# In-projection of a mixer layer: gate tiles first, convolution taps moved, first short taps on ScalarE

## What is computed

```python
h = rmsnorm(x, mix_norm[i]) @ w_in[i]            # 14 tiles of 128 columns in the kernel
y_mla  = mla_mixer(h[q 256], h[kv 128], h[k_pe 32])     # 8 heads of softmax attention
y_conv = conformer_conv_mixer(h[conv 512])       # a * sigmoid(g), depthwise conv of 31 taps, layernorm, silu
y_hy   = hyena_mixer(h[hy 768])                  # depthwise conv of 3 taps, two long convolutions by FFT
y = concatenate([rmsnorm(y_mla), rmsnorm(y_conv), rmsnorm(y_hy)])
x = x + y @ w_out[i]

# in mla_mixer
q  = rmsnorm(h_q, q_norm) @ w_qb
kv = rmsnorm(h_kv, kv_norm) @ w_kvb
```

## Time and profile before

| | |
|---|---|
| median of 3 runs | 3381.22 us (3379.67 to 3386.06) |
| the profiled execution's own time | 3378.02 us |
| its span, first to last instruction | 3376.2 us |
| busy: PE, DVE, ACT, POOL | 97%, 53%, 22%, 54% |
| in-projection and heads of layer 1 | 412 to 670 us of the span |
| the same of layer 2 | 1478 to 1737 us |

### The profile page before, as it was taken

The page is one execution under the profiler, slowest core; times in us unless marked ns, Lnnn a source line. Parts: engine busy times, 40 slices in busy tenths (PEclk is TensorE's granted clock), DMA queues, the critical chain, the costliest instruction groups (busy, mean ns, idle before and its releaser), DMA issues.

```text
span 3376.2 us, 43947 instructions
## 1 busy us (share of the span) xinstructions
PE 3259.0 (97%) x14466; PEld 2576.2 (76%) x14466; DVE 1803.6 (53%) x1969; ACT 744.3 (22%) x1260; POOL 1834.1 (54%) x1026
## 2 busy tenths in 40 slices
PE   8999998999999999999889999999999999999998
PEld 6788874478888788886457888788777777888886
DVE  7552268663312755138855331587768886753312
ACT  2110115522201111013532220111122322222200
POOL 5556651056666646663026666644455555666665
PEclk9999999999999999999999999999999999999999
DMA  4223320023233322331012232322222222223232
GB/s 156 79 76 99 112 81 26 7 82 99 94 99 98 111 75 88 100 110 59 13 33 93 94 99 95 120 75 69 69 85 66 73 68 75 90 91 99 94 99 81
DMA packets 77429, 281.24 MB, mean 83 GB/s; under 512 B 9382, under 2 KB 9766, under 8 KB 76776
## 3 DMA queue, kind: packets, MB, share of 16 engines
q1 hardware_dynamic: 74016, 268.58, 24.8%
q10 hardware_dynamic: 3272, 10.79, 1.0%
HBM read 277.24 MB, written 2.10 MB: 83 GB/s over the span
## 4 chain that ended last, share of the span: by engine, by line
PE 80%; DVE 14%; issue 4%; ACT 2%; DVEq 0%; DMA 0%; ACTq 0%; SPq 0%
PE bank L506 24%; PE bank L511 24%; PE bank L510 24%; DVE short L1925 1%; PE bank L730 1%; DVE y L1957 1%; PE bank L643 1%; DVE x_lo L1711 1%; DVE square_sum L1721 1%; DVE xbc L2264 1%; PE bank L813 1%; DVE scaled L2102 1%; PE bank L804 1%; PE bank L795 0%; PE bank L620 0%
## 5 line engine op out<-in xcount | busy, mean ns | idle before, releaser
L452 POOL TENSOR_SCALAR w_hi<-raw 128x1024 fp32r<-128x1024 f32 x504 | 555.3, 1102 | 1468.3 <-PE bank L506 1460.1
L455 POOL TENSOR_TENSOR w_lo<-raw,w_hi 128x1024 fp32r<-128x1024 f32 x504 | 1265.9, 2512 | 42.0
L506 PE MATMUL bank<-x_hi,w_hi 128*128 128x512 f32 x2896 | 1151.3, 398 | 47.4 <-DVE x_lo L1711 21.0
L511 PE MATMUL bank<-x_hi,w_lo 128*128 128x512 f32 x2896 | 1134.8, 392 | 0.0
L510 PE MATMUL bank<-x_lo,w_hi 128*128 128x512 f32 x2896 | 1133.9, 392 | 0.0
L506 PEld LDWEIGHTS bank<-x_hi,w_hi 128*128 128x128 f32 x2896 | 548.0, 189 | 184.5 <-issue 67.6
L511 PEld LDWEIGHTS bank<-x_hi,w_lo 128*128 128x128 f32 x2896 | 547.4, 189 | 116.4
L510 PEld LDWEIGHTS bank<-x_lo,w_hi 128*128 128x128 f32 x2896 | 548.2, 189 | 115.0 <-issue 4.1
L506 PE MATMUL bank<-hidden_hi,w_hi 128*128 (+1 forms) x880 | 342.3, 389 | 0.0
L510 PE MATMUL bank<-hidden_lo,w_hi 128*128 (+1 forms) x880 | 342.3, 389 | 0.0
L511 PE MATMUL bank<-hidden_hi,w_lo 128*128 (+1 forms) x880 | 342.3, 389 | 0.0
(11 more groups left out here) (379 smaller groups left out, 3238.5 us busy)
## 6 DMA issues: line engine op xcount, KB each, us to landing
raw<-in_w SPq DMA_DIRECT2D x504, 512.0 KB, 3.5
dft<-in_dft ACTq DMA_DIRECT2D x2, 1536.0 KB, 6.9
out<-x SPq DMA_DIRECT2D x4, 512.0 KB, 2.6
mask<-in_mask ACTq DMA_DIRECT2D x1, 1536.0 KB, 7.6
x<-in_x SPq DMA_DIRECT2D x2, 512.0 KB, 5.8
x<-in_x SPq DMA_DIRECT2D x1, 1024.0 KB, 8.6
filt_cos<-in_dft_filter ACTq DMA_DIRECT2D x2, 512.0 KB, 6.7
filt_sin<-in_dft_filter ACTq DMA_DIRECT2D x2, 512.0 KB, 8.2
```

The lines of the kernel that those rows point to most:

```text
L452: nc.gpsimd.tensor_scalar(w_hi[:, s % 2, :], raw[:, s, :], 1.0, 0.0, ALU.mult, ALU.add).then_inc(w_rounded, 1)
L455: nc.gpsimd.tensor_tensor(w_lo[:, s % 2, :], raw[:, s, :], w_hi[:, s % 2, :].bitcast(F32), ALU.subtract).then_inc(w_split, 1)
L506: first = nc.tensor.matmul(out, hi_w, hi, start=start, stop=False)
L511: return nc.tensor.matmul(out, lo_w, hi, start=False, stop=stop)
```

## The change

- The four gate tiles come first in the in-projection, ahead of kv, q and k_pe; the hyena tiles stay last.
- PE's small pieces move: the first `latent_sums` from behind tile 4 to behind tile 5, the others from tiles 5, 7, 8 into tiles 7, 9, 10.
- DVE does 15 long taps inside the in-projection where it did 10, at places spread between the tiles.
- The first tap of each of the six short tiles leaves DVE: ACT does it (`first_tap`, an ACTIVATE with scale and bias), and DVE waits for it (`gate_out`) before the second tap.
- `maximum(h, t)` does one long tap for heads 0, 1 and 2, and two from head 3 on.
- ACT: both sigmoids now come ahead of the latents' squares and roots.

```diff
@@ -900,9 +900,9 @@
                                                 start=True, stop=True)
                     last.then_inc(latent_spread, 1)
 
-                in_projection(IN_BLOCKS, {5: lambda: latent_spreads(1), 7: lambda: latent_sums(2),
-                                          8: lambda: latent_spreads(2)},
-                              {1: sum_squares, 4: lambda: latent_sums(1)})
+                in_projection(IN_BLOCKS, {7: lambda: latent_spreads(1), 9: lambda: latent_sums(2),
+                                          10: lambda: latent_spreads(2)},
+                              {1: sum_squares, 5: lambda: latent_sums(1)})
                 after(latent_scaled, 2)
                 pe.wait_ge(tile_free, c.at(tile_free) + 4)
                 signal_transposes(0)
@@ -1347,18 +1347,31 @@
                     act.wait_ge(gate_in, c.next(gate_in))
                     nc.scalar.activation(conv_s, conv_g, ACT.Sigmoid).then_inc(gate_out, 1)
 
-                def latent_norm(srcs, width):
+                def latent_squares(srcs):
                     act.wait_ge(norm_in, c.next(norm_in))
                     for i, src in enumerate(srcs):
                         nc.scalar.activation(square[:, i, :], src, ACT.Square).then_inc(norm_squared, 1)
+
+                def latent_square_root(width):
                     act.wait_ge(norm_sum, c.next(norm_sum))
                     nc.scalar.activation(latent_root[:], bank[SUM_BANK][:, 0:TT], ACT.Sqrt, bias=eps[:],
                                          scale=1.0 / width).then_inc(norm_rms, 1)
 
-                latent_norm([latent[:, 2, :]], P)
+                def first_tap(i):
+                    w, b = (layer_cols[:, n:n + 1] for n in (SHORT_W + i * SHORT, SHORT_B + i))
+                    act.wait_ge(gate_in, c.next(gate_in))
+                    nc.scalar.activation(short[:, i, :], short_pad[:, i, 0:T], ACT.Identity, bias=b, scale=w
+                                         ).then_inc(gate_out, 1)
+
                 conv_gate()
-                latent_norm([latent[:, i, :] for i in (0, 1)], 2 * P)
                 conv_gate()
+                latent_squares([latent[:, 2, :]])
+                latent_square_root(P)
+                latent_squares([latent[:, i, :] for i in (0, 1)])
+                first_tap(0)
+                latent_square_root(2 * P)
+                for i in range(1, 3 * CT):
+                    first_tap(i)
 
                 def signal(o):
                     for t in range(2):
@@ -1916,11 +1929,12 @@
                     link(nc.vector.tensor_tensor(long_pad[:, i, TAPS // 2:TAPS // 2 + T], conv_a, conv_s,
                                                  ALU.mult))
 
-                def short_tile(i):
+                def short_tile(i, meanwhile=lambda: None):
                     tile_out(short_pad[:, i, 1:1 + T])
+                    dve.sem_inc(gate_in, 1)
+                    meanwhile()
                     w = SHORT_W + i * SHORT
-                    link(nc.vector.tensor_scalar(short[:, i, :], short_pad[:, i, 0:T], col(w), col(SHORT_B + i),
-                                                 ALU.mult, ALU.add))
+                    dve.wait_ge(gate_out, c.next(gate_out))
                     for j in range(1, SHORT):
                         link(nc.vector.scalar_tensor_tensor(short[:, i, :], short_pad[:, i, j:j + T], col(w + j),
                                                             short[:, i, :], ALU.mult, ALU.add))
@@ -1936,7 +1950,7 @@
                                                               bank[SUM_BANK][:], ALU.mult, ALU.mult)
                     link(last, latent_scaled)
 
-                early = 10
+                early = 6
                 tap_order = [(0, j) for j in range(early)]
                 for j in range(TAPS):
                     tap_order.append((1, j))
@@ -1965,9 +1979,27 @@
                 def tap():
                     if taken[0] < 2 * TAPS:
                         long_tap()
-                for i in (2, 0, 1):
-                    tile_out(latent[:, i, :])
-                norm_squares(1)
+
+                gate_tiles()
+                gate_product(0)
+                long_taps(1)
+                tile_out(conv_a)
+                long_taps(3)
+                tile_out(conv_g)
+                dve.sem_inc(gate_in, 1)
+                long_taps(1)
+                gate_product(1)
+                long_taps(1)
+                tile_out(latent[:, 2, :])
+                norm_squares(1, lambda: long_taps(1))
+                long_taps(2)
+                tile_out(latent[:, 0, :])
+                long_taps(1)
+                latent_inverse()
+                long_taps(2)
+                tile_out(latent[:, 1, :])
+                norm_squares(2, lambda: long_taps(1))
+                latent_scale((2,), KV_NORM)
 
                 dve.wait_ge(tile_ready, c.next(tile_ready))
                 b = bank[RING[tile_no[0] % len(RING)]]
@@ -1977,23 +2009,14 @@
                 link(nc.vector.tensor_tensor(key_rope[V_DIM:QK, :], rope_c[V_DIM:QK, :], trig[V_DIM:QK, :], ALU.mult))
                 link(nc.vector.tensor_tensor(key_rope[V_DIM:QK, :], key_rope[V_DIM:QK, :], rope_d[V_DIM:QK, :],
                                              ALU.add))
+                short_tile(0, lambda: long_taps(1))
                 latent_inverse()
-                gate_tiles()
-                latent_scale((2,), KV_NORM)
-                gate_product(0)
-                norm_squares(2, lambda: long_taps(2))
-                long_taps(2)
-                latent_inverse()
-                long_taps(3)
+                short_tile(1, lambda: long_taps(1))
+                dve.sem_inc(signal_ready, 1)
+                short_tile(2)
                 latent_scale((0, 1), Q_NORM)
                 dve.sem_inc(latent_ready, 1)
-                gate_tiles()
-                long_taps(3)
-                gate_product(1)
-                short_tile(0)
-                short_tile(1)
-                dve.sem_inc(signal_ready, 1)
-                for i in range(2, 3 * CT):
+                for i in range(3, 3 * CT):
                     short_tile(i)
 
                 def fold(o, k):
@@ -2070,7 +2093,8 @@
                     nc.vector.reduce_max(row_shift[:, t:t + 1], bank[SCORE_BANKS[(4 * h + t) % 3]][:], AX_X, negate=True
                                          ).then_inc(row_ready, c.add(row_ready))
                     tap()
-                    tap()
+                    if h >= 3:
+                        tap()
 
                 def invert_sums(h):
                     dve.wait_ge(probs_ready, c.next(probs_ready, TT))
@@ -2582,10 +2606,10 @@
 def mixer_blocks(w_in, w_qb, w_kvb, w_out):
     q, kv, kpe, conv, hy = np.split(w_in, np.cumsum([256, 128, 32, 512]), 1)
     t = width_blocks(conv)
-    out = width_blocks(kv) + width_blocks(q)
+    out = [t[0], t[2], t[1], t[3]] + width_blocks(kv) + width_blocks(q)
     gap = np.zeros((D, ROPE), np.float32)
     out += width_blocks(np.concatenate([kpe, gap, swapped(kpe), gap], 1))
-    out += [t[0], t[2], t[1], t[3]] + width_blocks(hy)
+    out += width_blocks(hy)
     qb = w_qb.reshape(2, P, HEADS, QK)
     kvb = w_kvb.reshape(P, HEADS, NOPE + V_DIM)
     for g in range(2):
```

More of the change, by code:

```diff
@@ L93 @@
     "act": {"x_summed": 24, "sum_ready": 3, "gate_scaled": 44, "hidden_ready": 44, "x_updated": 24,
-           "layer_loaded": 96, "gate_in": 2, "ln_centered": 2, "ln_sum": 2, "norm_scaled": 10, "filt_angle":
+           "layer_loaded": 96, "gate_in": 8, "ln_centered": 2, "ln_sum": 2, "norm_scaled": 10, "filt_angle":
            4, "taps_decayed": 8, "taps_summed": 8, "spec_ready": 4, "signal_turned": 4, "norm_in": 3,
@@ L97 @@
            "latent_ready": 1, "mixed_copied": 8, "ln_out": 2, "freq_ready": 4, "tile_ready": 14},
-    "dve": {"pair_free": 44, "tile_free": 14, "dve_step": 151, "x_rounded": 24, "x_split": 24, "x_squared":
+    "dve": {"pair_free": 44, "tile_free": 14, "dve_step": 145, "x_rounded": 24, "x_split": 24, "x_squared":
            24, "x_summed": 24, "rms_ready": 3, "gate_ready": 44, "gate_scaled": 44, "up_ready": 44,
            "gate_activated": 44, "hidden_ready": 44, "hidden_rounded": 44, "hidden_split": 44, "out_ready":
-           24, "x_updated": 24, "layer_loaded": 96, "tile_ready": 14, "gate_out": 2, "ln_sum": 2,
+           24, "x_updated": 24, "layer_loaded": 96, "tile_ready": 14, "gate_out": 8, "ln_sum": 2,
            "ln_centered": 2, "norm_rms": 6, "norm_scaled": 10, "ln_out": 2, "filt_sum": 3, "filt_angle": 4,
```

## The result

The changed kernel takes 3387.66 us (median of 17 runs, 3385.39 to 3393.4), the kernel before 3382.1 (17 runs, 3378.22 to 3392.47). The ratio is 1.0014, with a 95% interval of 1.0008 to 1.0021: slower by 4.7 us on 3382, and by less than the 0.2% named in the prediction. The profiled execution took 3391.55 us, its span is 3389.5.

A forecast was written before the change was run, and what follows sets the result against it. PE has 80% of the chain, so DVE and ACT changes pay only where PE waits for DVE. Terms of +2.0 and +2.1 us on 3378.0 gave 3382, plus 3.2 to the median: 3385 us, range 3368 to 3396.

The forecast's parts named there:

- The new wait ahead of the first sums: In-projection: PE waits 3.5 us per layer for DVE's kv tile at the first latent_sums; an old 1.2 us goes.
- The list of held taps: In-projection: DVE taps end 0.54 us after POOL's piece, so PE goes on at 448.3 after arriving at 444.8.
- Behind the in-projection: From PE's last tile to the latent products: +0.6 us per layer, with one PE wait of 4.5 us.
- PE's clock: Behind two new waits per layer: falls of 2.0 us, 8 in 10, +3.2; old falls go, -1.7 and -1.6.
- The fall behind PE's wait in head 5: Head 5, wait made by late taps: a clock fall of 2.9 us, counted only in the slower-clock rival.
- One tap per row maximum: First heads, up to the row maximum of 550.91: -5.3 us per layer, bounds 0 and 7.4.
- The taps come back: Seven more taps due behind head 4's last row maximum: +2.9 us per layer, bounds 0 and 4.7.
- the gates weren't through in time: Rival at the first latent_sums: DVE reaches the kv tile by 443.5, PE doesn't wait; 3375 us, chance 0.25.
- the late taps weren't hidden: Rival in head 5: ACT's chain covers PE's wait; -5.8, 3379 us, chance 0.08.
- the heads gained all 5.3: Rival in the heads: they gain nothing, as scores and exponentials bound them; +10.6, 3396 us, chance 0.05.
- The clock as rival: Both new waits per layer and head 5's bring falls of 2.9 us each; 3393 us, chance 0.20.

The follow-up runs named there:

- experiment 4: Changed kernel with idle matmuls on PE in two waits per layer, ahead of the first latent_sums and of the frequencies; 0.9993 of the kernel before.
- Experiment 2: Changed kernel with the first tap of each short tile on DVE again, everything else as changed; 0.9982 of the kernel before.
- experiment 5: One tap per row maximum: undone in the changed kernel, 1.0034; alone in the kernel before, 1.0002; changed kernel with ten late taps in DVE's idle times, 0.9986.
- experiments 3 and 7: 3: changed kernel, first latent_sums one tile later, 1.0023 and 1.0000; 7: that plus v_time before mla_k and ten taps in DVE's idle times, 0.9940, variants 0.9916, 0.9948.
- experiments 1 to 4: Changed kernel with v_time before mla_k on ACT, 0.9978; first taps on DVE, 0.9982; first latent_sums one tile later, 1.0023 and 1.0000; idle matmuls in two waits, 0.9993.

## Why the prediction was right, and where it wasn't

The forecast, 3385 us and +0.1%, was right, and so was its shape: gains and losses of over 10 us that cancel. That it came so close is in part luck: for both layers together it had the clock up to 3.5 us too cheap and the rest 2 us too dear. Its terms, against what the runs showed per layer:

- **The new wait ahead of the first sums, +3.5 less 1.2 for the old.** Measured 2.75 for the wait, and 1.6 net: the in-projection takes 79.8 us with the clock held up (experiment 4) and 78.2 in the kernel before's order where nothing fell. PE arrived when predicted (448.13, that is 444.97 on the scale of before, against 444.8); DVE had the kv tile out about 0.6 us earlier. The list of held taps was right to 0.7 us.
- **Behind the in-projection, +0.6.** Measured 10.47 us without falls against 9.62, so +0.85, with one wait of 4.7 us where 4.5 was forecast. But the reason given was half wrong. The step read "So the lag that DVE loses, ACT adds", and it took the first taps on ACT for what removes the lag ("DVE now keeps up with PE"). Experiment 2 shows that the work moved to the front removes it, by 2.75 us per layer (9.6 to 6.86), while ACT's taps add 3.6 and a fall. The sum hid a part that was good by itself and one that only cost.
- **PE's clock, +3.2 less 1.7 and 1.6.** The term with the largest error. A fall was priced at 2.0 and taken 8 times in 10. In the profiled executions it came behind the 2.74 us wait in 12 of 12 cases and behind the 4.7 us wait in 10 of 10, at 1.6 to 3.4 us each. The changed kernel's four measure 7 us (experiment 4) where 6.4 was forecast, so the error stayed small there in the median. The fall behind PE's wait in head 5 was put at nothing in the sum. It was named in a rival only, which counts it once; it came in both layers, at 1.5 and 1.65 us (18.08 and 18.21 us from there to the conv mean's sum, against 16.55 where nothing falls). In all, the forecast had 3.1 us for the clock, and the mean granted clocks give up to 6.6.
- **One tap per row maximum, -5.3.** Measured -5.34 in both layers.
- **The taps come back, +2.9.** Measured +2.35 where nothing falls (71.5 against 69.15), and the wait for `out_spectrum` 2.59 us where "about 2.5" was said.

Without the clock these are 1.6 + 0.85 - 5.34 + 2.35 = -0.5 us per layer, against a forecast of +0.5. The rivals: PE waited at the sums, so the gates weren't through in time; the late taps weren't hidden (experiment 5); the heads gained all 5.3. The clock as rival had the mechanism right, and the medians lie between it and the forecast (+5.6 where the forecast had +4 and the rival +12).

## What to carry to other kernels

When a wait of PE is ended by ACT or DVE, read that engine's list just ahead of the releaser: here copies nobody was waiting for stood ahead of the one that PE waited for, and their order alone was worth 12 us, more than twice what the whole change moved. Work that is put off comes back at the next place without slack; put it into an idle time that the trace shows. Test parts of a change one by one and in pairs, since a part can cost in one order of the lists and gain in another, and price each new wait of PE with a fall of the clock, if it is like those here: of the changed kernel's three new waits (2.6 to 4.75 us), wherever they appear in these runs, 33 of 34 had one behind it.

## What the runs showed of the hardware

- A wait's length alone doesn't say whether the clock falls. Behind 2.74 us at the first sums it fell in 12 of 12 cases, behind 2.58 to 2.61 us at the second sums (experiments 3 and 7) in one of four, and there only two microseconds later. Behind PE's wait in head 5, 2.59 to 2.60 us and so no longer, it fell in 11 of 12 (the changed kernel and experiments 1 to 4). What differs ahead of them wasn't found.
- Work of no use in a wait pays for itself: six idle matmuls per layer took 0.2% off the kernel without moving a wait.
- ACT's tap of a tile of 128x512 takes 0.82 us, against 0.55 on DVE, and DVE waits 1.24 us for it from the end of its own preceding instruction.
